# Spatial gating in halves and tiles, a modulation chunk moved into the forgetting attention, mixer outputs turned tile by tile

## The reference, cut to what matters

```python
def sgu_mixer(h, w_in, ln_g, ln_b, w_s, b_s, w_out):          # layer 1
    u, v, z = jnp.split(h @ w_in, 3, axis=-1)
    u = jax.nn.gelu(u)
    v = layer_norm(jax.nn.gelu(v), ln_g, ln_b)
    w_causal = jnp.where(jnp.tril(jnp.ones((C, C), dtype=bool))[None], w_s, 0.0)
    mixed = jnp.einsum('gts,bnsgd->bntgd', w_causal, vc) + b_s.T[None, None, :, :, None]
    sg = u * mixed.reshape(B, S, SGU_WIDTH)
    return (sg * jax.nn.silu(z)) @ w_out

def first_block(x, c, ...):
    cond = jax.nn.silu(c)
    for i in range(DEPTH):                                    # 4 layers
        mod = (cond @ w_mod[i] + b_mod[i])[:, None, :]
        shift, scale, gate = jnp.split(mod, 3, axis=-1)
        h = rms_norm(x, norm_pre_g[i]) * (1.0 + scale) + shift
        o = mixer(h)                                          # gla, sgu, fox, gla
        x = x + gate * rms_norm(o, norm_post_g[i])
    ...
```

## Time and profile before

| what | value |
|---|---|
| median of 3 runs | 3364.41 us (3362.99 to 3364.54) |
| the profiled execution | 3364.1 us, of which the span is 3362.3 us |
| PE busy | 3137.1 us, 93% of the span |
| DVE, ACT, POOL busy | 49%, 36%, 9% |
| chain that ended last | PE 72%, DVE 16%, ACT 8%, DMA 2%, issue 2% |
| mean TensorE clock granted | 0.973 of full speed |

### The profile page before, as it was taken

How to read it: one execution, slowest core, us unless ns; L and a number is a source line. 1 busy time by engine, 2 the same in 40 slices (tenths; PEclk the granted TensorE clock), 3 DMA queues, 4 the chain that set the end, 5 groups by cost and what they waited for, 6 DMA issues and landing times.

```text
span 3362.3 us, 55127 instructions
## 1 busy us (share of the span) xinstructions
PE 3137.1 (93%) x23594; PEld 2548.0 (76%) x23594; DVE 1663.3 (49%) x2678; ACT 1195.4 (36%) x2165; POOL 307.3 (9%) x308
## 2 busy tenths in 40 slices
PE   7989988989999899899997899999999988989998
PEld 5767767756776787788885578888888776678886
DVE  3255435345534646676765565333334446653444
ACT  4315325446431554422223444211112425642222
POOL 1020010000002000144432001000000101000000
PEclk9999999989999999999998999999999989999999
DMA  5283232260226321232121003212121314042231
GB/s 211 83 324 98 81 123 80 80 247 19 90 76 244 109 99 58 77 104 89 65 74 42 26 14 70 81 51 76 51 76 51 99 50 77 1 99 77 100 113 63
DMA packets 176062, 306.58 MB, mean 91 GB/s; under 512 B 20326, under 2 KB 41639, under 8 KB 175561
## 3 DMA queue, kind: packets, MB, share of 16 engines
q1 hardware_dynamic: 148064, 278.71, 24.7%
q0 software_dynamic: 3712, 12.74, 1.4%
q10 hardware_dynamic: 24041, 11.60, 1.4%
HBM read 294.87 MB, written 6.80 MB: 90 GB/s over the span
## 4 chain that ended last, share of the span: by engine, by line
PE 72%; DVE 16%; ACT 8%; DMA 2%; issue 2%; POOL 0%; ACTq 0%; DVEq 0%; SPq 0%
PE psum L425 17%; PE psum L426 17%; PE psum L427 17%; PE psum L2372 5%; PE psum L944 3%; PE psum L583 2%; DVE weights_r L369 2%; PE psum L963 2%; DVE small L1108 2%; ACT feat L692 1%; DVE arena L861 1%; DVE x_lat L864 1%; PE psum L978 1%; PE psum L2364 1%; PE psum L2436 1%
## 5 line engine op out<-in xcount | busy, mean ns | idle before, releaser
L369 DVE TENSOR_TENSOR weights_r<-weights,weights_r 128x2048 fp32r<-128x2048 f32 (+2 forms) x168 | 364.0, 2186 | 527.1 <-ACT weights_r L360 527.0
L425 PE MATMUL psum<-feat_r,weights_r 128*128 128x512 f32 (+1 forms) x1552 | 542.8, 350 | 10.9 <-DVE feat_r L722 4.9
L425 PE MATMUL psum<-weights_r,feat_r 128*128 128x512 f32 (+2 forms) x1344 | 527.0, 392 | 17.9 <-DVE weights_r L369 12.5
L426 PE MATMUL psum<-feat_r,weights_r 128*128 128x512 f32 (+1 forms) x1552 | 540.8, 348 | 0.0
L427 PE MATMUL psum<-feat_r,weights_r 128*128 128x512 f32 (+1 forms) x1552 | 539.9, 348 | 0.0
L360 ACT ACTIVATE weights_r<-weights 128x2048 fp32r<-128x2048 f32 (+2 forms) x168 | 302.9, 1824 | 619.4 <-DMA weights<-in_w_ffn_gate 207.8
L427 PE MATMUL psum<-weights_r,feat_r 128*128 128x512 f32 (+2 forms) x1344 | 520.4, 387 | 0.0
L426 PE MATMUL psum<-weights_r,feat_r 128*128 128x512 f32 (+2 forms) x1344 | 520.1, 387 | 0.0
L425 PEld LDWEIGHTS psum<-feat_r,weights_r 128*128 128x128 f32 x1552 | 294.4, 190 | 56.1 <-issue 5.2
L426 PEld LDWEIGHTS psum<-feat_r,weights_r 128*128 128x128 f32 x1552 | 294.5, 190 | 37.1
L427 PEld LDWEIGHTS psum<-feat_r,weights_r 128*128 128x128 f32 x1552 | 294.2, 190 | 37.5
(11 more groups left out here) (478 smaller groups left out, 4417.2 us busy)
## 6 DMA issues: line engine op xcount, KB each, us to landing
weights<-in_w_mod SPq DMA_DIRECT2D x48, 2048.0 KB, 12.9
weights<-in_gla_w_in SPq DMA_DIRECT2D x24, 1024.0 KB, 7.3
weights<-in_w_ffn_gate SPq DMA_DIRECT2D x20, 1024.0 KB, 7.4
weights<-in_w_ffn_up SPq DMA_DIRECT2D x20, 1024.0 KB, 5.1
...
```

Source lines behind the costliest of these rows:

```text
L369: dve.e.tensor_tensor(WEI_r[:, s * SLOT:s * SLOT + n], WEI_t[:, s * SLOT:s * SLOT + n], WEI_r[:, s * SLOT + HALF:s * SLOT + HALF + n].bitc ...
L425: pe.e.matmul(ps, lh, rh, start=first, stop=False)
L426: pe.e.matmul(ps, lh, rl, start=False, stop=False)
```

## The change

Three things are changed.

1. The spatial gating is reordered. DVE takes the moments of v by halves as the gelus come, and the root of all four tiles is one instruction. ACT splits u1 before it waits for the moments. POOL multiplies by halves and tiles. PE mixes tiles 0 to 2 and turns tile 0 before it mixes tile 3; DVE mixes tiles 0 and 1, and 2 and 3 between the low parts. The moments get buffers of their own for each tile.
2. The side in spatial gating (the gate third of the modulation of layer 2) goes to the forgetting attention, which now has five.
3. For the ends of layers 0, 1 and 3 the transposes go tile by tile, both halves of a tile together, and each waits only for DVE's mark of its tile.

```diff
-SIDES_BEGIN, SIDES_GLA, SIDES_SGU, SIDES_FOX, SIDES_GDN = 2, {0: 6, 3: 5}, 1, 4, 6
+SIDES_BEGIN, SIDES_GLA, SIDES_SGU, SIDES_FOX, SIDES_GDN = 2, {0: 6, 3: 5}, 0, 5, 6
...
+    def by_tile(tag):
+        return tag in (("end", 0), ("end", 1), ("end", 3))
+    def feat_order(tag, tiles):
+        return [(h, t) for t in tiles for h in range(2)] if by_tile(tag) else [(h, t) for h in range(2) for t in tiles]
+    def pe_to_feat(pe, tag, y, tiles, before=None):
+        if not by_tile(tag):
+            pe.wait_ge(*A.of((tag, "in")))
+            pe.wait_ge(*V.of((tag, "in")))
+        for h, t in feat_order(tag, tiles):
+            if before is not None and (h, t) in before:
+                before[h, t]()
+            if by_tile(tag):
+                pe.wait_ge(*V.of((tag, "in", t)))
...
     def act_to_feat(act, tag, tiles, by_columns=False):
         A.mark((tag, "in"))
-        act.wait_ge(*V.of((tag, "in")))
+        if not by_tile(tag):
+            act.wait_ge(*V.of((tag, "in")))
+        for h, t in feat_order(tag, tiles):
...
+    def dve_to_feat(dve, tag, tiles, by_columns=False, before=None):
+        if not by_tile(tag):
+            V.mark((tag, "in"))
+            dve.wait_ge(*A.of((tag, "in")))
+        for h, t in feat_order(tag, tiles):
+            if before is not None and (h, t) in before:
+                before[h, t]()
...
                 dve.e.scalar_tensor_tensor(zh, K.at[at][:, 0:GDV], ss[:, h:h + 1], zh, ALU.mult,
                                            ALU.mult).then_inc(*V.put(K.frees(V, at)))
+            V.mark((("end", i), "in", c))
             dve_gla_side(dve, i, LEVELS + 1 + c)
...
     def pool_sgu(pool):
-        pool.wait_ge(*A.of((T, "z")))
-        for t in LAT:
-            pool.e.tensor_tensor(s_z[:, t, :], s_z[:, t, :], s_u[:, t, :], ALU.mult).then_inc(*G.put((T, "uz", t)))
+        for n0 in (0, NMAX):
+            for t in LAT:
+                pool.wait_ge(*A.of((T, "z", n0, t)))
+                half = s_z[:, t, n0:n0 + NMAX]
+                pool.e.tensor_tensor(half, half, s_u[:, t, n0:n0 + NMAX], ALU.mult).then_inc(*G.put((T, "uz", n0, t)))
...
     def pe_sgu(pe):
-        for n in range(SIDES_SGU):
-            pe_side(pe)
         pe_side(pe, False)
-        for t in LAT:
+        for t in LAT[:3]:
+            pe_sgu_mix(pe, t)
...
     def act_sgu(act):
-            if part == "u":
-                for t in LAT:
-                    act.wait_ge(*V.of((T, "moments", t)))
-                    act.chain()
-                    act.e.activation(s_mv[:, 2:3], s_mv[:, 1:2], ACT.Sqrt, bias=eps_col).then_inc(*A.put((T, "root", t)))
             for n0 in (0, 512):
                 act_take(act)
+                if (part, n0) == ("u", 0):
+                    act.wait_ge(*V.of((T, "moments")))
+                    act.chain()
+                    act.e.activation(s_mv[:, :, 2:3], s_mv[:, :, 1:2], ACT.Sqrt, bias=eps_col).then_inc(*A.put((T, "root")))
...
     def dve_sgu(dve):
-        dve_take(dve)
-        dve_take(dve)
+        for h, n0 in enumerate((0, NMAX)):
+            dve_take(dve)
+            for t in LAT:
+                dve.wait_ge(*A.of((T, "v", n0, t)))
+                dve.e.bn_stats(s_st[:, t, 6 * h:6 * h + 6], s_v[:, t, n0:n0 + NMAX]).then_inc(*V.put())
...
+        dve_take(dve)
+        dve.wait_ge(*A.of((T, "root")))
...
+            if t == 0:
+                dve_take(dve)
         V.mark((T, "ln"))
-        for n in range(4):
+        for n in range(2):
             dve_take(dve)
-        for n in range(SIDES_SGU):
-            dve_side(dve)
         dve_side(dve, False)
+        for t in LAT[:2]:
+            dve_sgu_mix(dve, t)
...
-        pe_to_feat(pe, T, y, LAT)
+        pe_to_feat(pe, T, y, LAT, {(0, 1): lambda: pe_sgu_mix(pe, 3)} if i == 1 else None)
...
-        dve_to_feat(dve, T, LAT)
+        dve_to_feat(dve, T, LAT, before={(0, t - 1): lambda t=t: dve_sgu_mix(dve, t) for t in (2, 3)} if i == 1 else None)
```

103 lines of the change are left out of this document (44 added, 59 removed).

## The result

The changed kernel takes 3341.34 us (median of 3 runs, 3337.23 to 3344.57); before it was 3364.41. The ratio of the two is 0.992 with a 95% interval of 0.9904 to 0.9935: 27 us less, between 22 and 32 (the two medians alone are 23 us apart). The forecast was 3343, 21.4 us less, with a range down to 3338. The median lies in that range; by the ratio (0.992 x 3364.41 = 3337.5) the gain is larger than the range allowed for, by half a microsecond. The direction came as forecast and so did the places where time went; the sizes of three terms did not, that of the end of layer 0 first. The profiled execution of the changed kernel is the one of 3344.57 us; its span is 3342.8, against 3362.3 before.

A forecast was written before the change was run, and what follows sets the result against it. PE, 93% busy with 72% of the chain, was taken as the bound. Terms -2.25 - 6.6 - 14.7 + 4.6 - 2.2 = -21.15 from 3364.1, plus 0.3 to the median, gave 3343 us; range 3338 to 3354.

The forecast's parts named there:

- End of layer 0: Turning tile by tile lets the product and gate column come earlier: 2.25 us off, bounds 0 and 3.8.
- PE's wait for v0: Sign at the next layer's first weights: the wait grows from 1.06 to about 2.6 us.
- Split of u1: Spatial gating: PE's 3.74 us wait and 2.9 us of low clock go, 6.6 us off.
- z1's end to the product: Spatial gating's end: 28.96 us until the output product becomes 14.3, so 14.7 us off; 9.3 at the other end.
- POOL beside the splits: Spatial gating: POOL's halves beside DVE's weight splits cost at most 11.4 us, spread over splits with slack; taken as 0.
- The fifth side: Forgetting attention: the added side lies on the path, 4.6 us on; bounds 3.6 and 8.
- End of layer 3: Gate, and the context load issued behind it, come earlier: 2.2 us off, bounds 0 and 3.1.
- PE's wait for the context: Sign at the end of layer 3: the wait of 3.13 us grows by 1 us.
- (c): Rival: both ends carry fully and the side fills PE's gaps; 24.7 us off, 3339.7; chance 0.04.
- (a): Rival: turning gives nothing outside layer 1, gate and context load being slower by as much; 3347.7; chance 0.11.
- (b): Rival: attention's side costs 8, mixing keeps 0.55 us an instruction with low clock behind; 3352; chance 0.11.
- (d): Rival: slower than before, the fifth weight pair not in when PE reaches attention unit 32; 3371.6; chance 0.04.

The follow-up runs named there:

- the ends alone: Kernel before, with only the ends of layers 0 and 3 turned tile by tile: 3361.27 us, ratio 0.9974.
- the side alone: Kernel before, with only the fifth side moved from spatial gating to the forgetting attention: 3364.1 us, ratio 0.9985.

## Why the prediction was near, and where it failed

**End of layer 0: the term that was too small.** Forecast -2.25, measured -3.9, -4.2 and, with the ends alone, -4.1. The gate column came 2.7 us earlier, not 2.25: DVE's eight low parts took 4.87 us, 0.61 each, and I had used 0.64 and a later start. The larger part of the error is that I held the gate's way through DRAM at 16.8 us, the one value that the trace of before showed. From column to residual it was 15.58, 15.3 and 15.4 in these kernels. In four others with the new turning the residual followed the column by 14.6 to 14.8 us; in three of those it did not wait for the gate at all. So 14.6 us is what the output product and the norm behind it need, and the stage can then be 4.5 us shorter. The bound that I gave was 3.8, from a product that starts at 270.4; it started at 269.67 on the axis of before, 4.5 us earlier than 274.18. Of the twelve executions with the new turning eleven lie beyond that bound, at 3.9 to 4.5 us; one is at 3.5. PE's wait for v0 grew to 1.64 and not to the forecast 2.6, for the same reason.

**Split of u1: right.** -6.8 in every trace that has it, the wait and the low clock both gone; with that edit alone the same.

**z1's end to the product: 1 us better than forecast, and for the reasons given for the most part.** 13.33 and 12.96 us against the forecast 14.3, and 12.96 or 12.97 in all six other executions with this order in layer 1; the mixing went at 0.41 to 0.43 an instruction as in the row taken for it, and the last of it ended 12.1 us behind z1's end where I had 12.9. What was wrong is the role of the weaving: by my own numbers, mixing whole until 7.9 and turning 5.4 gives 13.3, and I did not do that sum. The run gave 12.63. I had left the clock out: the changed kernel's first execution had some six slow matmuls at the product's start, the second had none (its first matmul took 0.48 us). That the term came out at -14.5 in the first execution is luck, 1 us too little against 1.2 us of clock.

**POOL beside the splits: right to take as 0, with the row misread.** I read 11.35 us for four as 2.84 each. It was three of 2.35 and one of 4.39. One of the halves in the changed kernel met a split of DVE at 439.81 and took 2.92 us instead of 1.29; it was POOL that was held, with time to spare.

**The fifth side: the size of the first execution, too large for most.** Forecast +4.6. It was +4.6 in one execution and with the side alone, +2.7 in the other; over the ten traces with five sides in the attention it is 2.7 to 3.7 in eight and 4.6 in these two. My bound of 3.6 for a side that fills gaps of PE was thus near the usual size.

**End of layer 3: near in size, and the larger thing overlooked.** -2.6 and -2.7 against -2.2. I saw that the context's load is issued behind the gate's write and took 2.2 us of the gate's earlier column for it, but did not ask how long the load takes by itself. I had PE's wait for the context grow by 1 us, and it grew by 2.75. The wait of 3.13 us was a sign that a megabyte needed 15 us where DMA moved 359 GB/s in the attention, 2.9 us for as much.

Of the rivals, (c), that the ends carry fully and the side fills gaps, was the nearest: it holds for layer 0 and for the side in most executions. (a) and (b) fell, and so did (d): the fifth pair was in time, and the 3.02 us stop behind the last side is the z block's split as before. The reason given for (b), that each stop of over 3 us in the trace is followed by slow matmuls, was not so throughout: at 2615.88 of the kernel before eight transposes take 1.06 us behind a stop of 3.21, and the same eight at 1156.93 take 1.94 behind 3.13.

What carried the time out of the range is then no single term. With -4.2, -6.8, -16.0, +3.1 and -2.7, the sizes that come most often in these traces or lie in their middle, the sum is -26.6, beside the 27 of the ratio: layer 0 gives 2 us of the difference, the side 1.5, the way to the product 1.3.
